# Output projection in seven block products, with its activations kept in DRAM

## The reference

```python
x = x + 0.5 * swiglu_ffn(rms_norm(x, norm_ffn1_g), w_ffn1_up, w_ffn1_down)
u_ssm, v_conv, gate_logits = split(rms_norm(x, norm_mix_g) @ w_in)
y_a = glu_val * sigmoid(glu_gate)      # of gelu(s5_ssm(u_ssm)) @ w_ssm_glu
y_b = conformer_conv(v_conv)           # depthwise, LayerNorm, silu, then @ w_conv_pw
g_a, g_b = split(sigmoid(gate_logits))
x = x + (g_a * y_a + g_b * y_b) @ w_out            # the output projection
x = x + 0.5 * swiglu_ffn(rms_norm(x, norm_ffn2_g), w_ffn2_up, w_ffn2_down)
out = rms_norm(x, norm_final_g)
```

## Time and profile before

| | |
|---|---|
| median of three runs | 2199.1 us |
| span of the profiled execution | 2196.5 us |
| the profiled execution's own time beside its span | not listed apart; the span is 2.6 us under the median of the runs |
| PE busy | 2151.8 us, 98%, 10239 matmuls |
| DVE, ScalarE (ACT), GpSimd (POOL) busy | 77%, 43%, 29% |
| chain that ended last | PE 82%, DVE 10%, ACT 2%, DMA 2%, issue 2% |
| window of the output projection, 1450.6 to 1544.8 us | PE 90.94, DVE 44.52, ACT 41.41, POOL 0.60 us busy; DMA share 0.41 |

### The profile page before, as it was taken

How to read it: one execution, slowest core, us unless ns; L and a number is a source line. 1 busy time by engine, 2 the same in 40 slices (tenths; PEclk the granted TensorE clock), 3 DMA queues, 4 the chain that set the end, 5 groups by cost and what they waited for, 6 DMA issues and landing times.

```text
span 2196.5 us, 31579 instructions
## 1 busy us (share of the span) xinstructions
PE 2151.8 (98%) x10239; PEld 1777.8 (81%) x10239; DVE 1685.9 (77%) x2123; ACT 943.0 (43%) x1552; POOL 633.5 (29%) x717
## 2 busy tenths in 40 slices
PE   7999999999999999999999999999999999999997
PEld 6788788787878888888888888887878888888886
DVE  5877877879995999999998659364597777665557
ACT  5455555544455122222224125044355555544444
POOL 2887645969990000000000420000024442000000
PEclk9999999999999999999999999999999999999999
DMA  5334776478774345544545622563256664337754
GB/s 172 79 118 158 261 245 208 143 263 298 258 265 153 103 140 154 154 134 149 156 127 166 215 82 88 186 210 106 72 173 211 225 212 157 104 115 264 229 192 172
DMA packets 307649, 379.60 MB, mean 173 GB/s; under 512 B 27761, under 2 KB 200401, under 8 KB 307440
## 3 DMA queue, kind: packets, MB, share of 16 engines
q1 hardware_dynamic: 287024, 306.27, 43.5%
q0 software_dynamic: 18800, 67.85, 9.4%
q10 hardware_dynamic: 1744, 4.46, 0.5%
HBM read 258.42 MB, written 120.08 MB: 172 GB/s over the span
## 4 chain that ended last, share of the span: by engine, by line
PE 82%; DVE 10%; ACT 2%; DMA 2%; issue 2%; SPq 0%; DVEq 0%; ACTq 0%
PE PU L1405 10%; PE PU L1406 10%; PE PU L1407 10%; PE PU L1345 9%; PE PU L1346 9%; PE PU L1347 9%; PE PD L1280 3%; PE PD L1281 3%; PE PD L1282 3%; PE PU L1280 2%; PE PU L1281 2%; PE PU L1282 2%; DVE Alo L2086 2%; DVE Dlo L2083 1%; PE PD L1481 1%
## 5 line engine op out<-in xcount | busy, mean ns | idle before, releaser
L1345 PE MATMUL PU<-Hhi,Whi 128*128 128x512 f32 x896 | 352.5, 393 | 0.4 <-issue 0.2
L1347 PE MATMUL PU<-Hhi,Wlo 128*128 128x512 f32 x896 | 349.2, 390 | 0.0
L1346 PE MATMUL PU<-Hlo,Whi 128*128 128x512 f32 x896 | 349.1, 390 | 0.0
L2500 DVE SCALAR_TENSOR_TENSOR XT<-XT,wq 128x1024 f32<-128x1024 f32 x240 | 311.9, 1299 | 8.2
L1345 PEld LDWEIGHTS PU<-Hhi,Whi 128*128 128x128 f32 x896 | 168.3, 188 | 38.1 <-issue 3.9
L1347 PEld LDWEIGHTS PU<-Hhi,Wlo 128*128 128x128 f32 x896 | 168.3, 188 | 35.3
L1346 PEld LDWEIGHTS PU<-Hlo,Whi 128*128 128x128 f32 x896 | 168.4, 188 | 34.7 <-issue 0.7
L1405 PE MATMUL PU<-Hhi,Dhi 128*128 128x512 f32 x480 | 187.0, 390 | 0.0
L1407 PE MATMUL PU<-Hhi,Dlo 128*128 128x512 f32 x480 | 186.9, 389 | 0.0
L1406 PE MATMUL PU<-Hlo,Dhi 128*128 128x512 f32 x480 | 186.9, 389 | 0.0
L1280 PE MATMUL PD<-Dhi,Ahi 128*128 128x512 f32 x352 | 138.1, 392 | 3.8 <-DVE Alo L2086 3.7
(11 more groups left out here) (405 smaller groups left out, 5142.5 us busy)
## 6 DMA issues: line engine op xcount, KB each, us to landing
TAB<-in_w_ffn_down POOLq DMA_DIRECT2D x44, 512.0 KB, 5.0
d_sb<-TAB POOLq DMA_DIRECT2D x44, 512.0 KB, 4.0
Wraw<-in_w_ffn_up SPq DMA_DIRECT2D x80, 256.0 KB, 3.8
XT<-in_w_ffn_up SPq DMA_DIRECT2D x80, 256.0 KB, 4.5
d_sa<-XT SPq DMA_DIRECT2D x80, 256.0 KB, 2.4
Wraw<-in_w_in SPq DMA_DIRECT2D x32, 512.0 KB, 5.2
d_act<-G SPq DMA_DIRECT2D x48, 256.0 KB, 2.7
WRd<-d_sb SPq DMA_DIRECT2D x44, 256.0 KB, 4.1
```

The source lines that it names most:

```text
L1345: mm(o_, Whi[s][:, side, k, :], Hhi[:, k, hs[h]], start=k == 0, stop=False)
L1346: mm(o_, Whi[s][:, side, k, :], Hlo[:, k, hs[h]], start=False, stop=False)
L1347: last = mm(o_, Wlo[s][:, side, k, :], Hhi[:, k, hs[h]], start=False, stop=k == KT - 1)
L2500: stt(CVb, z_, w_, CVb, ALU.mult, ALU.add).then_inc(m["conv"], 1)
```

## The change

The output projection gets the scheme of the down projections: seven products of four steps t (couples of 128-row blocks), 28 steps for 32. For that:

- Every merged tile is stored in DRAM (`d_m`). DVE forms four block sums of each pair of tiles (`merged_sums`), which SP stores in `d_ms`; for the first three pairs they are formed in the space of Alo, for the last in TAB. Seven transfers of 256 KB a pair.
- GpSimd loads w_out, forms four weight sums for each couple (16 instructions of 128x512) and stores them in `d_wo`. This stands right behind its variance sums.
- Each step loads a weight block and an activation block, and ScalarE and DVE split both. The ring has four slots for each. Copies of merged tiles into Hhi, Hlo fall away.
- The first four splits on DVE stand around the last pair's merge: steps 0 to 2 ahead of the first half, step 3 ahead of the second.
- The residual rows of half 0 are loaded behind the loads of the first three merged tiles, those of half 1 behind the storing of all sums.
- The additions to the residual use `gather`, 32 instructions for 16.
- The squares of half 0 are taken behind products 2 and 5 of the row, its scaled rows between the splits of the last product. That product runs its four steps for row blocks 0, 1 and then for 2, 3. The first turn of half 0 stands in the second of these, the second turn in the first matmuls of the FFN.

The core of the diff. The table that sets the number of steps:

```diff
-OUTP = Proj(KT, 7 * FI, None, 7, 7 * (FI - 1))
+OT = KT // 2
+OUTP = Proj(OT, 7 * FI, 7, 7 * (FI - 1))
```

SP, behind `pw_io(n)` and `load_pair` of each pair n:

```diff
-                    load_step(OUTP, 0, t)
+                    load_out_weights(0, t)
+            else:
+                for a, h in ((1, 0), (0, 0), (1, 1)):
+                    store_merged(n - 1, a, h)
+                store_merged_sums(n - 1)
+        sp.wait_ge(m_st, 16 * 7 * (OT - 1))
+        for t in range(OT - 1):
+            load_merged(0, t)
+        load_rows(0)
+        sp.wait_ge(b_["m"], 4 * OT - 2)
+        store_merged(OT - 1, 1, 0)
+        store_merged(OT - 1, 0, 0)
+        sp.wait_ge(m_st, 16 * (7 * OT - 5))
+        load_merged(0, OT - 1)
+        for t in range(OT):
+            load_merged(1, t)
+        sp.wait_ge(b_["m"], 4 * OT)
+        store_merged(OT - 1, 1, 1)
+        store_merged_sums(OT - 1)
+        for t in range(OT):
+            load_out_weights(1, t)
+            if t == 1:
+                sp.wait_ge(m_st, 16 * 7 * OT)
+                load_rows(1)
+        for p in range(2, 7):
+            for t in range(OT):
+                load_merged(p, t)
+                load_out_weights(p, t)
```

GpSimd, behind the variance sums:

```diff
+        for t in range(OT):
+            for i in range(2):
+                if t:
+                    pool.wait_ge(sb_st[i], TAKEN0[FFN2][i] - 16 * (OT - t))
+                pool.dma_start(WOr[:, i, :], w_out[0][(2 * t + i) * P:(2 * t + i + 1) * P]).then_inc(pool_ld[i], 16)
+            for i in range(2):
+                pool.wait_ge(pool_ld[i], 16 * (TAKES + t + 1) + (0 if i else TABLES0[FFN2]))
+            (b12, b11), (b22, b21) = [halves(WOr[:, i, :]) for i in range(2)]
+            step(g.tensor_tensor(b11, b12, b11, ALU.subtract))
+            step(g.tensor_tensor(b12, b22, b12, ALU.subtract))
+            step(g.tensor_tensor(b22, b22, b11, ALU.subtract))
+            step(g.tensor_tensor(b21, b22, b21, ALU.subtract))
+            for i in range(2):
+                pool.dma_start(d_wo[t, 2 * i:2 * i + 2].rearrange("a p n -> p a n"), rows_p(WOr[:, i, :])).then_inc(sb_st[i], 16)
```

TensorE:

```diff
+        def out_proj():
+            for p in range(6):
+                for t in range(OT):
+                    proj_step(OUTP, p, t)
+            for js in ((0, 1), (2, 3)):
+                for t in range(OT):
+                    proj_step(OUTP, 6, t, js, js[-1] == 3)
+                    if (js[0], t) == (2, 1):
+                        turn("nf2", 0, 0)
```

ScalarE, first in `slot_free`:

```diff
             elif S is OUTP:
                 act.wait_ge(m["u_full1"], KT)
+                act.wait_ge(m_st, 16 * 7 * (OT - 1))
...
+        def out_proj():
+            for p in range(1, 6):
+                for t in range(OT):
+                    split_step(OUTP, p, t)
+                if p == 2:
+                    quadrant(OUTP, 0, 1, 1, 0)
+            quadrant(OUTP, 0, 0, 4, 4)
+            split_step(OUTP, 6, 0)
+            split_step(OUTP, 6, 1)
+            act.wait_ge(*norm_at("nf2", "rs", RS_STEPS["nf2"]))
+            act.wait_ge(x_st, 16 * (J + 4))
+            scaled_rows("nf2", OUTP, 0, (0, 1))
+            split_step(OUTP, 6, 2)
+            scaled_rows("nf2", OUTP, 0, (2, 3))
+            split_step(OUTP, 6, 3)
+            quadrant(OUTP, 1, 0, 5, 8)
+            turned("nf2", 0, 0)
+            quadrant(OUTP, 1, 1, 6, 12)
+            turned("nf2", 0, 1)
```

DVE:

```diff
+        def merged_sums(n):
+            if n < OT - 1:
+                for i in range(2):
+                    dve.wait_ge(sb_st[i], TAKEN0[FFN2][i])
+                if n:
+                    dve.wait_ge(m_st, 16 * 7 * n)
...
+            dve.wait_ge(b_["m"], 4 * n + 4)
+            tt(s1, a21, a22, ALU.add).then_inc(m_sum, 1)
+            tt(s3, a11, a21, ALU.subtract).then_inc(m_sum, 1)
+            dve.wait_ge(m_sum, 4 * n + 1)
+            tt(s2, s1, a11, ALU.subtract).then_inc(m_sum, 1)
+            dve.wait_ge(m_sum, 4 * n + 3)
+            tt(s4, a12, s2, ALU.subtract).then_inc(m_sum, 1)
...
         for n in range(KT // 2):
-            if n == KT // 2 - 1:
-                for t in range(RING):
-                    split_step(OUTP, 0, t)
             dve.wait_ge(b_["gb_ld"], 64 * (n + 1))
             for h in range(2):
+                if n == KT // 2 - 1:
+                    for t in range(RING - 1) if h == 0 else (RING - 1,):
+                        split_step(OUTP, 0, t)
...
-                if n == KT // 2 - 1:
-                    lo_half(h, b_["m_hi"], b_["m_lo"])
+            merged_sums(n)
             split_pair(R_PW + n + 2, n % 2)
-        proj(OUTP, "nf2")
-        added_all(OUTP, 3)
+        out_proj()
```

More of the change, by code:

```diff
@@ L78 @@
 ADDS = 4 * sum(len(to) for to in D_TO.values())
-X0 = {FFN1: 0, OUTP: ADDS, FFN2: ADDS + 16}
-D_ADDS = {S: [X0[S] + 4 * sum(len(D_TO[x]) for x in D_ORD[:p]) for p in range(8)] for S in (FFN1, FFN2)}
+X0 = {FFN1: 0, OUTP: ADDS, FFN2: 2 * ADDS}
+D_ADDS = {S: [X0[S] + 4 * sum(len(D_TO[x]) for x in D_ORD[:p]) for p in range(8)] for S in (FFN1, OUTP, FFN2)}
 KEPT = (FI + 1, 2 * FI)
@@ L438, in alone @@
         eng.sem_inc(passed, 1)
-    def proj_phase(eng, S, p, step, behind={}):
-        def one(t):
-            step(S, p, t)
-            if t in behind:
-                behind[t]()
-        for t in range(S.steps):
-            one(t)
     @block.sync
@@ L1659, in slot_free @@
                 act.wait_ge(m["u_full1"], KT)
+                act.wait_ge(m_st, 16 * 7 * (OT - 1))
+                for i in range(2):
+                    act.wait_ge(sb_st[i], TAKEN0[FFN2][i])
             else:
@@ L2168, in proj, with out_proj @@
[L2168 to L2180 removed]
+        def out_proj():
+            for p in range(1, 6):
+                for t in range(OT):
+                    split_step(OUTP, p, t)
+                if p in (1, 3):
+                    dve.wait_ge(mx_ld[p // 2], 32)
+                for j in range(4):
+                    gather(OUTP, p - 1, j)
+            split_step(OUTP, 6, 0)
+            row_scale("nf2", 0)
+            for t in range(1, OT):
+                split_step(OUTP, 6, t)
+            for j in range(4):
+                gather(OUTP, 5, j)
+            gather(OUTP, 6, 0)
+            gather(OUTP, 6, 1)
+            turned("nf2", 0, 0)
+            gather(OUTP, 6, 2)
+            gather(OUTP, 6, 3)
+            turned("nf2", 0, 1)
@@ L2182, in gather @@
+        halves_of = lambda k: (XT[:, k, 0:HW], XT[:, k, HW:L])
         def gather(S, p, j):
```

221 lines of the change are left out of this document (93 added, 128 removed).

## The result

The changed kernel takes 2229.2 us (median of four runs, 2225.6 to 2233.2) against 2199.1: the ratio is 1.0132, 95% interval 1.0115 to 1.0148. It is slower, as forecast, but by 30.1 us and not by 14, and the range ended at 2223. A second set of runs gave 2228.2 and 1.0125 (1.0110 to 1.0140).

A forecast was written before the change was run, and what follows sets the result against it. TensorE at full granted clock was taken to fill the span. The output projection's +7.3 us and GpSimd's +7 beside DVE made +14.3 on 2199.1, forecasting 2213 us, with a range of 2200 to 2223.

The forecast's parts named there:

- Matmuls, -10.9: Output projection: 336 matmuls for 384, so 48 fewer at 0.2266 us each, -10.9 us.
- The chain through DRAM: Output projection: storing and reloading merged tiles and sums makes PE wait 1.8, 4.0, 9.4 and 2.7 us in products 0 and 1.
- the tail: End of the output projection: late scaled rows, step splits and additions make PE wait 4.2 us together in product 6.
- The third step: Product 1 of the projection: third weights, queued behind a 2 MB row load, land near 1482.6; PE waits 2.7 us.
- The granted clock should stay at its upper level, 2.4 GHz, as throughout: Whole kernel: PE was expected to keep its full granted clock, with no time added for slow matmuls.
- GpSimd's part: Ahead of the pointwise convolution: GpSimd's 16 additions slow DVE's layer-norm row, 0.8 us each; +7 us, bounds 0 and 13.
- a sixth for reads of PSUM: Layer-norm stretch: the 13 us that additions cost DVE was cut by a sixth, the estimated share of its PSUM reads.
- another 1 for the last round: Ahead of the pointwise convolution: 7 us taken instead of 8, since GpSimd's last round may fall behind 1363.
- GpSimd free: Rival: projection costs +7.3 us, GpSimd's additions nothing, as DVE's gaps and breaks between rounds take them; 2207 us, chance 0.25.
- neither costs much: Rival: with landings at lower bounds the projection costs +1 us and GpSimd 0 to 3; 2201 us, chance 0.16.
- The full lock: Rival: each GpSimd addition shuts DVE out for its whole 1.39 us, +20 on top of +7.3; 2226 us, chance 0.06.
- Faster: Rival: merged tiles reach the projection before PE needs them, only 4.2 us of late waits remain; -10, 2189 us, chance 0.07.

The follow-up runs named there:

- the idle and filled kernels: Kernel before with eight pauses of PE in the output projection, left idle (2225.5 us) or filled with 22 unused matmuls each (2239.5 us).
- a part alone: Kernel before plus only GpSimd's four rounds of block sums of w_out, which nobody reads: 2217.1 us, ratio 1.0074.
- the mark run: The changed kernel once more, unaltered, as reference for the runs beside it on the same chip: 2228.2 us.
- run 8: Not a label: in "in the mark run 8 follow" the 8 counts slow distances; the run is the changed kernel once more, 2228.2 us.
- the reordered chain: Changed kernel with the last pair's first half merged before the weight splits and small loads issued ahead of both row loads: 2216.2 us, ratio 1.0070.
- the runs with three late rounds: Changed kernel with GpSimd's last three rounds started at the convolution's first half of inputs: 2211.5 us; with the chain's issue order also changed: 2200.5 us.

## Why the prediction was wrong

**Matmuls, -10.9: right.** 336 of them, 0.227 apart wherever nothing waits.

**The chain through DRAM: places right, one size off.** Forecast against measured, in us after PE is free:

| | forecast | measured |
|---|---|---|
| wait at the first step | 1.8 | 1.26 |
| wait at the fourth step | 4.0 | 4.86 |
| product 1's first matmul | 26.1 | 27.0 |
| its third step | 34.2 | 38.1 |
| waits in product 6 (the tail) | 4.2 | 2.6 |

The third step was mis-sized. I let the weights land 8 us after the second row load was issued; they landed 11.7 us after it (11.25 from their own issue), and the step came 3.9 us late. The run that moved the row load shows where this comes from: its wait is gone.

**The failed step: "The granted clock should stay at its upper level, 2.4 GHz, as throughout".** That sentence carried a term of zero, where the profile has 6.6 us on the path. The waits that I had added up myself are what takes the clock down. Of the 52 slow distances 19 lie before the last two points that the chain sets, and are swallowed by the waits there. 33 are on the path: 7 at the convolution, 14 behind the third weights, 12 in the tail, together 6.6 us. The stage's miss is then 3.9 for the weights, 5.2 for 26 slow distances, -1.6 for the shorter tail waits and a rest of 1.1, of which 0.7 are the small starts that the stage had before and that my sum left out: 8.6, which is 110.3 less the forecast 101.7. GpSimd's part missed by 6.6 of waits (13.6 for 7) and the 1.4 of clock. So the clock (5.2 + 1.4) and GpSimd's price (6.6) have equal shares in the whole miss.

The stretch that I read could not show this term: the longest wait of PE there is 2.21, followed by matmuls at the upper level. The trace of the kernel before does show it elsewhere, in the first FFN, where eight distances of 0.427 follow a wait of 2.03 us (PE's timeline, then the window):

```profile
397.93 0.62 PE L1405 MATMUL PU<-T3hi,Ahi 128*128 128x512 f32 x1 [2.03 <-DVE G L2294]
398.35 0.63 PE L1406 MATMUL PU<-T3lo,Ahi 128*128 128x512 f32 x1
```

```profile
396.00:402.00 6.00, 4.07 (x11) 3.24 (x12) 3.57 (x5) 1.86 (x3) 5.22 (x9) 0.72 0.39 141
```

A slice of the page is 55 us long, and its digit stays 9 over this dip. So "as throughout" was a wrong reading of the earlier trace rows. The Trainium skill ("TensorE: Matmul & The Clock Gate", Part 1: The HAM clock gate) has the rule that half the clock is what idling brings; the idle and filled kernels here agree with it, 30 slow distances against none. Not every idle time brings it: behind the 11.79 us that PE waits at the start of the kernel before, the granted clock is 1.00. I had not weighed the rule, since the page's row of before has nothing but 9s.

**GpSimd: mechanism right, price wrong.** Forecast 7, and 0 to 13 as bounds; measured 13.6 of waits in the changed kernel and 1.4 of clock, 17 as a part alone. Two steps of the term failed. The price of an addition was read from five long taps as 0.8; with VectorE instructions of 0.69 us it is 0.98. And I took off a sixth for reads of PSUM and another 1 for the last round. The six instructions that read PSUM and a gate product in that stretch (`G<-G,PU`) did keep their 0.68 to 0.69 us, one of them, at 1328.04, while an addition ran (1327.53, 1.63 us). But the additions fell beside other instructions, and the last round fell wholly ahead of the convolution. To this comes the wait for a gate tile, which I did not have. The rule of the Trainium skill that I cited ("SBUF — State Buffer", Who interferes with whom) comes out better than I made it: the rows show the two engines alternating, one instruction each. Only the sum that I drew from it was too high, +20, because VectorE's own 0.69 are not lost and about one round fell into gaps.

**The sum.** -10.9 - 3.3 (the old waits) + 19.3 of waits in the projection + 9.0 of its 45 slow distances + the same rest of 1.1 gives 15.2, and 15.9 is measured. With 15.0 at the convolution it is 30.9, for 30.1 by the medians. The forecast of the time was the sum of two terms with the right sign, both about half as large as they are.

**The rivals.** "GpSimd free" is refuted by the part alone, and "neither costs much" by both stages. The full lock gave 2226 and was nearest in time, for a wrong reason: its chain was +7.3. "Faster" was never near in this form; product 1 came 16 us after PE could have begun it. What stays open is why 12 slow matmuls stand in the tail of one profile of the changed kernel and none in that of the second, at waits of 2.0 and 0.6 in the one, 2.7 and 1.5 in the other.

## What to carry to other kernels

When a change puts waits on the path of a TensorE that so far hardly idled, price each wait of a few us with a second term for the slow matmuls behind it, and let it count only up to the next point that something other than PE sets. Look for such matmuls behind the waits that the kernel already has, in the timeline and not in the page's slices. Before work is given to an idle GpSimd, ask which instructions VectorE runs at that very time and whether VectorE is late there; sixteen additions ahead of the convolution cost 15 us, and four ahead of it with twelve beside it cost nothing there. All sixteen beside it did not fit. In a chain through DRAM the order of issue comes first: 2 MB loads ahead of small ones, and a merge behind three splits, were together worth 12 us, as much as the eighth of the matmuls that the scheme saves (10.9).

## What the hardware showed that was not expected

- Slow matmuls follow short waits, too. In the kernel before 8 slow distances follow a wait of 2.03 us, in the mark run 8 follow one of 1.9 us, and in the reordered chain 8 follow one of 1.87; in the runs with three late rounds none follow waits of 3.08 and 3.28. From 3.7 us on, every wait of these runs in the projection or ahead of the convolution had 6 to 14 behind it.
- The price does not grow with the wait: 7 slow distances behind 12.75 and 12.79 us, 7 behind 21.87, 11 behind 4.86, 14 behind 3.70.
- A VectorE instruction with a single tile as input (and two columns of scalars) is held up beside GpSimd's additions as well. In VectorE's timeline of the changed kernel, inside and outside a round:

```profile
1366.65 1.51 DVE L2700 TENSOR_SCALAR XT<-XT,vecs 128x512 f32<-128x512 f32 x1
...
1369.75 0.53 DVE L2700 TENSOR_SCALAR XT<-XT,vecs 128x512 f32<-128x512 f32 x1
```
